# A two-network kernel on one core: the entry's norm ahead of the filter's layers, the latent's tiles ahead of the context's behind the even product, modulation halves ahead of their weight units

## The reference

```python
for layer in range(DEPTH):                 # 0 even, 1 odd
    sh, sc, ga = adaln(c or c_ctx, w_mod[layer], b_mod[layer])   # silu(cond) @ w_mod + b_mod, in three parts
    h = rms_norm(x, g_pre[layer]) * (1 + sc) + sh                # for the latent and for the context
    # even: h @ e_w_in -> Hyena branch (short convolution, long convolution with a filter made by
    #       a small sine network, sin(freq * (z @ w1 + b1)) and so on), and attention with rotary q, k
    # odd:  h @ o_w_in -> q, k, v, o, z of an mLSTM
    y = mixer(h) @ w_out
    x = x + ga * rms_norm(y, g_post[layer])
```

## Time and profile before

| | us |
|---|---|
| median of 3 runs (lowest, highest) | 2029.33 (2027.41, 2030.05) |
| the profiled execution, own time | 2031.51 |
| its span, first to last instruction | 2029.7 |
| PE busy | 1884.0 |
| DVE busy | 1129.2 |
| ACT busy | 857.6 |
| mean granted clock of PE | 0.961 |

### The profile page before, as it was taken

One profiled execution on the slowest core, in us unless ns is written; L12 is line 12 of the kernel. 1 busy time (PEld: TensorE's weight loads), 2 busy tenths in 40 slices (PEclk: granted clock), 3 DMA queues, 4 the chain that ended last, 5 costly groups with the idle time before them and its releaser, 6 DMA issues. The chain is left out here.

```text
span 2029.7 us, 24208 instructions
## 1 busy us (share of the span) xinstructions
PE 1884.0 (93%) x9322; PEld 1512.7 (75%) x9322; DVE 1129.2 (56%) x2019; ACT 857.6 (42%) x1353; POOL 48.9 (2%) x53
## 2 busy tenths in 40 slices
PE   5999999899897889997878999999999999999997
PEld 2666688777685767885557788879987878779986
DVE  3534266566533733346985677566654667466644
ACT  3313345312223533254444465645643555635542
POOL 1000000000000000001000001000000001000000
PEclk8989999999998989998889999999999999999999
DMA  9305511211233422264004434455555444445552
GB/s 333 136 32 193 201 54 51 73 62 42 82 106 115 145 79 83 87 200 149 1 1 166 162 113 152 145 166 166 187 187 187 155 134 135 145 165 168 187 197 83
DMA packets 113786, 265.12 MB, mean 131 GB/s; under 512 B 4695, under 2 KB 8056, under 8 KB 113480
## 3 DMA queue, kind: packets, MB, share of 16 engines
q1 hardware_dynamic: 109408, 248.47, 37.0%
q0 software_dynamic: 3008, 10.85, 1.6%
q10 hardware_dynamic: 1256, 4.25, 0.6%
HBM read 262.51 MB, written 1.05 MB: 130 GB/s over the span
## 5 line engine op out<-in xcount | busy, mean ns | idle before, releaser
L144 DVE TENSOR_TENSOR qw_rest<-weights,qw_lead 128x1024 fp32r<-128x1024 f32 (+2 forms) x428 | 520.5, 1218 | 584.3 <-ACT qw_lead L309 583.5
L309 ACT ACTIVATE qw_lead<-weights 128x1024 fp32r<-128x1024 f32 (+2 forms) x428 | 448.3, 1049 | 706.0 <-PE psum L153 671.9
L153 PE MATMUL psum<-qw_lead,b_h_lead 128*128 128x512 f32 (+1 forms) x480 | 199.5, 416 | 10.1 <-DVE hT L2682 5.4
L153 PE MATMUL psum<-qw_lead,b_h_rest 128*128 128x512 f32 (+1 forms) x480 | 188.8, 393 | 0.0
L153 PE MATMUL psum<-qw_rest,b_h_lead 128*128 128x512 f32 (+1 forms) x480 | 188.3, 392 | 0.0
L153 PE MATMUL psum<-e_h_lead,qw_lead 128*128 128x512 f32 x320 | 144.8, 453 | 6.0 <-PEq L118 5.7
L153 PE MATMUL psum<-b_h_lead,qw_lead 128*128 128x256 f32 x512 | 145.2, 284 | 0.0
L153 PE MATMUL psum<-b_h_rest,qw_lead 128*128 128x256 f32 x512 | 144.9, 283 | 0.0
L153 PE MATMUL psum<-b_h_lead,qw_rest 128*128 128x256 f32 x512 | 144.9, 283 | 0.0
L153 PE MATMUL psum<-e_h_lead,qw_rest 128*128 128x512 f32 x320 | 126.7, 396 | 0.0
L153 PE MATMUL psum<-e_h_rest,qw_lead 128*128 128x512 f32 x320 | 125.9, 393 | 0.0
(11 more groups left out here) (460 smaller groups left out, 3533.2 us busy)
## 6 DMA issues: line engine op xcount, KB each, us to landing
weights<-in_w_in SPq DMA_DIRECT2D x48, 1024.0 KB, 5.0
weights<-in_o_w_in SPq DMA_DIRECT2D x32, 1024.0 KB, 5.3
weights<-in_w_mlp_up SPq DMA_DIRECT2D x32, 1024.0 KB, 5.5
weights<-in_w_mlp_down SPq DMA_DIRECT2D x32, 1024.0 KB, 4.8
weights<-in_e_w_in SPq DMA_DIRECT2D x26, 1024.0 KB, 5.2
weights<-in_w_mod SPq DMA_DIRECT2D x24, 1024.0 KB, 6.6
weights<-in_e_w_out SPq DMA_DIRECT2D x8, 1024.0 KB, 4.8
weights<-in_o_w_out SPq DMA_DIRECT2D x8, 1024.0 KB, 4.9
```

The source lines that it names most:

```text
L144: return eng.tensor_tensor(self.rest[at], src, self.lead[at].bitcast(F32), ALU.subtract)
L153: mm = nc.tensor.matmul(out, l, r, start=start and i == 0, stop=stop and i == 2)
L309: self.core.nc.scalar.activation(self.buf.lead[self.at(u)], self.raw(u), ACT.Copy).then_inc(self.lead_ready, 1)
```

## The change

It does five things, all of them to the order of work.

1. At the entry the first sine, the squares of x, the second sine, the squares of ctx and the root come ahead of the first modulation row's copy on ACT; the second layer's product comes ahead of the second modulation half on PE; the tables' DMAs from POOL wait for the second row and not for the first.
2. In `e_q2` and `e_gatt` each raw half stands ahead of its split unit, not behind it: the places of `mods1` are 15.9 + 2n, `late` is 0.05.
3. In the stream, the first half of `o_q` stands ahead of the four `mod1g` halves; `floor` is now 34.0 from the last unit of `e_out` on.
4. `Residual` and `OddNorm` are cut into pieces with places of their own: the two latent tiles go through square, root, add and norm first; the context's tiles are released from their banks and left until the latent's transposes stand. A Sqrt on a constant comes ahead, at 29.1.
5. The second `Residual`, behind the odd product, uses the same pieces.

```diff
     def cols(name, w, starts, width=BANK, chunks=None):
...
                 for q in range(2):
+                    if chunk:
+                        mod_half(*chunk, q)
                     units.append((at, q * 2 * width, 2, width, True))
-                    if chunk:
-                        l, j = chunk
-                        units.append((len(halves), 0, 4, BANK, False))
...
-    mods("mod1g", 1, (4, 5))
     w = a["o_w_in"][0]
-    cols("o_q", w, (0, 512))
-    cols("o_k", w, (OD_K, OD_K + 512))
+    first["mod1g"] = len(units)
+    first["o_q"], early = len(units) + 4, len(halves)
+    halves.append([(w[0:BANK, 0:BANK].rearrange("(k p) n -> p k n", p=P), 0, 4, BANK)])
+    for j in (4, 5):
+        for r in range(2):
+            mod_half(1, j, r)
+    for h, at in ((early, 0), (early, 1), (len(halves), 0), (len(halves), 1)):
+        units.append((h, at * 2 * BANK, 2, BANK, True))
+    halves.append([(w[BANK:2 * BANK, 0:BANK].rearrange("(k p) n -> p k n", p=P), 0, 4, BANK)])
+    cols("o_q2", w, (512,))
...
@@ Filter.layers, args, sines
-        yield -4.4
+        yield -4.95
...
-            yield (-6.1, -4.3)[i]
+            yield (-6.1, -4.9)[i]
...
-            yield (-4.7, -3.0)[i]
+            yield (-5.5, -4.85)[i]
...
@@ Enter.stats, norms
-            yield (-4.2, -4.1, -2.9, -2.8)[t]
+            yield (-5.2, -5.1, -4.8, -4.75)[t]
...
-        yield -2.6
+        yield -4.65
...
-        yield -2.75
+        yield -4.7
...
-        yield -2.4
+        yield -4.6
...
 class Residual(Stage):
+    def squares(self, act):
+        for t in range(self.tiles):
+            yield self.places[t][0]
+            act.wait_ge(w.chunk, self.dense.product_at(2 * t + 1))
+            if t:
+                act.wait_ge(self.squared, t)
+            nc.scalar.activation(self.junk.rearrange("p (j n) -> p j n", j=2), self.bank(t), ACT.Square, accum_out=self.ssq[:, t:t + 1]).then_inc(self.squared, 1)
+
+    def roots(self, act):
+        yield self.places[0][0] - 1.5
+        self.core.nc.scalar.activation(self.root[:, 0:1], self.core.ident[:, 0:1], ACT.Sqrt)
+        for t in range(self.tiles):
+            yield self.places[t][1]
...
+    def means(self, dve):
+        for t in range(self.tiles):
+            yield self.places[t][1] - 0.05
...
+    def products(self, dve):
+        for t in range(self.tiles):
+            yield self.places[t][2]
...
+    def adds(self, dve):
+        for t in range(self.tiles):
+            yield self.places[t][3]
...
@@ OddNorm.turns
-                pe.wait_ge(self.residual.read, 2 * s + 2)
+                pe.wait_ge(self.residual.read, 2)
...
@@ even_layer, first phase
-    filt.others_first = lambda pool: pool.wait_ge(mods0.rows_out, 1)
+    filt.others_first = lambda pool: pool.wait_ge(mods0.rows_out, 2)
...
-    mods1 = Mods(core, "m1_", r, [(0, 4), (0, 5), (1, 0), (1, 1), (1, 2), (1, 3)], raws, [17.7 + 2 * n for n in range(12)],
+    mods1 = Mods(core, "m1_", r, [(0, 4), (0, 5), (1, 0), (1, 1), (1, 2), (1, 3)], raws, [15.9 + 2 * n for n in range(12)],
...
-    run_stages(core, [... Feed(core, (dense,), (mods0, mods1), prime=(-1.9, -1.2, 3.0), late=(first["e_q2"], 2.1), floor=(first["e_kv"], 3.1)),
+    run_stages(core, [... Feed(core, (dense,), (mods0, mods1), prime=(-1.9, -1.2, 3.0), late=(first["e_q2"], 0.05), floor=(first["e_kv"], 3.1)),
...
@@ even_layer, last phase
+    res = Residual(core, "er_", dense, NT, [0, 0, 1, 1], ...,
+                   [(30.6, 30.7, 30.9, 31.1), (30.8, 31.2, 31.4, 31.6), (31.3, 32.6, 32.7, 34.7), (31.5, 32.9, 33.3, 34.9)], ...)
+    mods2 = Mods(core, "m2_", r, [(1, 4), (1, 5)], ..., [32.1, 32.2, 32.3, 32.4], ..., late=3.0)
+    norm = OddNorm(core, res, odd.h, ...,
+                   st[:, 16:32], [(32.0, 32.2, 32.8), (32.3, 32.5, 33.2), (35.0, 35.2, 35.6), (35.3, 35.5, 35.8)], ((33.5, 0.15), (36.0, 0.3)))
-    run_stages(core, [dense, source, res, norm, mods2, qk, Feed(core, (dense, qk), (mods2,), floor=(where["units"][-3], 33.1)),
+    run_stages(core, [dense, source, res, norm, mods2, qk, Feed(core, (dense, qk), (mods2,), floor=(where["units"][-1], 34.0)),
...
@@ odd_layer, its Residual
+                   [(at, at + 0.6, at + 0.9, at + 0.9), (at + 0.6, at + 1.2, at + 1.5, at + 1.5)])
```

More of the change, by code:

```diff
@@ L1446, in __init__ @@
         self.squared, self.meaned, self.rooted, self.read, self.x_ready = s("squared"), s("meaned"), s("rooted"), s("read"), s("x_ready")
-        self.vector, self.scalar = (self.adds,), (self.squares,)
+        self.vector, self.scalar = (self.means, self.products, self.adds), (self.squares, self.roots)
     def bank(self, t):
@@ new lines, in roots @@
+    def roots(self, act):
[3 more added lines that the diff above has]
+            yield self.places[t][1]
+            act.wait_ge(self.meaned, t + 1)
+            self.core.nc.scalar.activation(self.root[:, t:t + 1], self.mean[:, t:t + 1], ACT.Sqrt).then_inc(self.rooted, 1)
+    def means(self, dve):
+        for t in range(self.tiles):
+            yield self.places[t][1] - 0.05
+            dve.wait_ge(self.squared, t + 1)
+            self.core.nc.vector.tensor_scalar(self.mean[:, t:t + 1], self.ssq[:, t:t + 1], 1.0 / D, EPS, ALU.mult, ALU.add).then_inc(self.meaned, 1)
@@ new lines, in products @@
+    def products(self, dve):
+        core, nc, two = self.core, self.core.nc, lambda z: z.rearrange("p (j n) -> p j n", j=2)
+        for t in range(self.tiles):
+            yield self.places[t][2]
+            dve.wait_ge(self.rooted, t + 1)
+            core.dve_chain(dve, nc.vector.reciprocal(self.rec[:, t:t + 1], self.root[:, t:t + 1]))
+            if t >= 2:
+                dve.wait_ge(self.x_ready, t - 1)
+            nc.vector.scalar_tensor_tensor(out=two(self.tmp[t % 2]), in0=self.bank(t), scalar=self.rec[:, t:t + 1], in1=two(core.ga[:, self.gate_of[t], :]),
+                                           op0=ALU.mult, op1=ALU.mult).then_inc(self.read, 1)
@@ L1601, in even_layer @@
     u = first["e_q2"]
-    items.append(Item(**span(range(u, u + 8, 2), 16.0, 2.0), groups=tokens(BANK), src=r.h, **heads_out(BANK)))
+    items.append(Item(**span(range(u + 1, u + 8, 2), 16.0, 2.0), groups=tokens(BANK), src=r.h, **heads_out(BANK)))
     u = first["e_gatt"]
@@ L1605, in even_layer @@
     for i in range(2):
-        items.append(Item(**span(range(u + 8 * i, u + 8 * i + 8, 2), 24.0 + 8 * i, 2.0), groups=feats, src=r.h,
+        items.append(Item(**span(range(u + 8 * i + 1, u + 8 * i + 8, 2), 24.0 + 8 * i, 2.0), groups=feats, src=r.h,
                           act=lambda g, i=i: silu(4 * i + g)))
@@ L1612, in even_layer @@
     dense = Dense(core, "e_in_", items, (0, 1, 2, 3), outs_ready=x_turned)
-    raws = [first["e_q2"] + 1 + 2 * n for n in range(4)] + [first["e_gatt"] + 1 + 2 * n for n in range(8)]
+    raws = [first["e_q2"] + 2 * n for n in range(4)] + [first["e_gatt"] + 2 * n for n in range(8)]
     def second_free(pe):
@@ L1798, in odd_queries @@
     items = []
-    for name, chan0, dst, width, dt in (("o_q", 0, odd.qT, SEQ, 1.06), ("o_k", 8, odd.kT, 2 * SEQ, 2.0)):
+    for names, chan0, dst, width, dt in (("o_q", "o_q2"), 0, odd.qT, SEQ, 1.06), (("o_k", "o_k2"), 8, odd.kT, 2 * SEQ, 2.0):
         act_out, dve_out = out_of(dst, chan0)
```

87 lines of the change are left out of this document (36 added, 51 removed).

## The result

Median 2052.39 us (2050.97 to 2053.67, four runs) against 2029.03 for the kernel before on the same chip (2027.41 to 2030.05, four runs): ratio 1.0116, 95% interval 1.0098 to 1.0133, or 23.4 us more. The prediction said 2045.5, slower. The direction and the mechanism held, and the size was 7 us short.

The account below looks back on a forecast made before the run. PE was taken as the bound, busy 1884.0 of 2029.7 us. Terms -4.8 + 2.8 + 19.0 + 7.0 - 4.2 - 4.0 + 0.4 = +16.2 us on the median 2029.3 gave 2045.5 us, range 2030 to 2056.

Parts of the forecast that it names:

- The five waits of ACT: First phase: row's copy falls behind a take waiting for a DMA; PE stands 3.9 us in five pairs, 19 us lost.
- Rival A: First phase: the copy is not held, as the half lands within 2.3 us of the sums' start; 2019.5 us, chance 0.15.
- The clock after such stalls: First phase: lower clock behind each 3.9 us stall costs 1.4 us, 7 us lost in all; bounds 0 and 10.
- Rival B: First phase: the stalls come but the clock holds; 2038.5 us, chance 0.2.
- The first raw half waits for the filter: At the filter's end: PE stands 2.8 us at the first raw half, waiting for DVE's last filter step.
- The entry: Kernel start: ACT starts on h at 28.3, 4.8 us earlier; gain no less than 3, no more than 5.5.
- the last turn of the shifts and scales stays at 26.1 to 27.1: Kernel start: first row's copy is delayed, but this later turn on PE keeps its time, 26.1 to 27.1 us.
- The end of that phase: First phase's end: less work behind the last product gains 2.2 us, a PE hardly cooled 2.0 more; together 4.2.
- Behind the even product: After the even product: transposes start 11.6 us earlier, later waits leave some 4 us gain; bounds 1 to 8.
- The second residual: Behind the odd product: root and reciprocal of tile 1 come later, behind DVE's add of tile 0; loss 0.4 us.
- Rival C: Entry and tail give nothing, as late filter tables and waits for the gate eat both; 2054.3 us, chance 0.07.
- rival D: First phase: stalls of half the size, from a DMA alone on the queues, tail at its best; 2028 us, chance 0.1.

Follow-up runs that it names:

- e1: Kernel after with `late` of the first phase 0.3, not 0.05, so the weight half's take stands behind the row's copy: 2030.16 us, ratio 1.0008.
- e7: Kernel after with 22 unused 128x128 products ahead of PE's wait for the row in the first five pairs: 2046.11 us, ratio 1.0082.
- e6: Kernel after with `late` of the first phase 2.1 and DVE's last filter step at 16.35, not 17.0: 2021.24 us, ratio 0.9957.
- e5: Kernel after with `late` of the first phase 2.1, as before, so the take stands behind the row's and heads' copies: 2023.00 us, ratio 0.9969.
- e2: Kernel after with the first phase's part undone (raw halves behind their split units, places 17.7 + 2n, `late` 2.1): 2021.94 us, ratio 0.9958.

## Why the prediction was right in kind and short in size

**The five waits of ACT: right.** 5 x 3.9 - 0.6 = 19.0 us predicted, 19.2 measured (3.6, 3.5, 3.9, 3.7, 4.5). The half's way from the sums to ACT, 6.2 us in the earlier trace rows, took 6.35 in the wait shown (193.19 to 199.54). e1 shows that the order of take and copy makes them: with it turned, none is left. Rival A (the copy isn't held) needed a landing within 2.3 us of the sums' start, and ACT's take never started before 6.15 (6.5, 6.4, 6.35, 6.15, 6.9). From SP's issue to the take it was 5.0 to 5.8 us, 5.2 at the third wait. The Trainium skill (DMA: Bandwidth & Descriptors, Anatomy of one DMA) gives a fit that came to an estimate of 4.4 us and waits of 3.2; the waits measured 3.8 on average, so the row was the better guide, and the fit too low here. The page states that fit for copies issued from GpSimd; these are issued from SP.

**The clock after such stalls: the term that was mis-sized.** Predicted 7 us (1.4 each), bounds 0 and 10; measured 12.4 (1.5 to 3.4 each), beyond the upper bound. The step that failed is "I take 1.4 for each stall of 3.9 us": one stall's price put on all five. The 1.4 came from six products after one wait at 553.96, and for that stall it was right, as the level was back at full directly behind them (two windows of before; the last three numbers are PEclk, DMA share, GB/s):

```profile
553.00:557.00 4.00, 3.04 (x8) 2.42 (x9) 3.69 (x5) 2.89 (x7) 0.00 (x0) 0.57 0.96 370
557.00:560.00 3.00, 3.00 (x15) 2.45 (x14) 0.03 (x1) 0.00 (x0) 0.00 (x0) 1.00 1.03 411
```

The row at 517.91 says 1.6 (5.37 less twice 1.88). But behind the 2.59 us of the earlier trace rows before lost some 2.5, and behind the 10.35 of the earlier trace rows some 2.7. Of the five stalls after, the first two cost what the earlier trace rows shows (1.7 and 1.5), the other three 2.5 to 3.4, since the level stayed low for longer. The third, from 201 us on:

```profile
201.00:208.00 7.00, 6.87 (x20) 5.42 (x20) 4.55 (x7) 0.08 (x1) 0.00 (x0) 0.52 0.07 22
208.00:211.00 3.00, 3.00 (x17) 1.69 (x17) 1.22 (x1) 1.06 (x1) 0.00 (x0) 0.99 0.23 29
```

The length of a wait doesn't tell which price it pays: 3.6 us cost 1.7, and 3.7 cost 2.5. e7 shows the cause. The Trainium skill (TensorE: Matmul & The Clock Gate, Part 1) says that idleness brings the throttled rate back, and the runs agree (that the clock can fall without idle time as well is told below). Rival B (the clock holds) fell.

**The first raw half waits for the filter: right, a little short.** Predicted 2.8 us, measured 3.9. PE came at 135.8 and not at 138.2, since the filter's sums didn't lose the clock this time, and DVE's step ended only 1.6 us earlier than I had it (139.5 against 141.1). e6 shows that DVE's order makes it. What I left out is that the clock was low there before as well (behind L834, 140 to 147 us): by the products' shifts the wait cost 2.5 us net, from -6.1 to -3.6.

**The entry: too much.** Predicted 4.8, measured 3.4 at ACT's first step on h, and 2.8 from 80 us on. In the timeline of PE after:

```profile
20.65 1.87 PE L915 MATMUL psum<-small,e_qT 128*128 128x2 f32 x8 [2.24 <-ACT e_qT L897]
22.45 3.64 PE L887 MATMUL psum<-weights,cond 128*32 128x512 f32 x16
26.80 1.87 PE L915 MATMUL psum<-small,e_qT 128*128 128x2 f32 x8 [0.71 <-ACT e_qT L897]
28.53 1.95 PE L1036 MATMUL psum<-ident,x_res 128*128 128x128 f32 x8
```

Here "the last turn of the shifts and scales stays at 26.1 to 27.1" failed. It starts 0.7 us later, and takes 1.87 us where before, at the full level, it took 1.05. I had named the wait for the first row's copy (behind the root) and not what it does to the second. That copy itself came at 20.0 and not at 19.3: ACT's first square started at 12.0, where I had x land at 11.4. The low level is read from the durations. PEclk is given as 1.00 from 0 to 37 us, yet the matmuls of L153 take 0.63 us each until 36.6, and 0.39 from 37.7 on.

**The end of that phase: nearly.** Predicted 4.2, measured 3.7 (from +29.4 to +25.7). The idle time ahead of the next phase fell from 2.59 to 0.94 us, and the low clock behind it (2.5 us of PE's busy time before, from 241.24 on) is gone. A new wait of 1.1 us at its second step takes a part back. e5 shows that this gain hangs on the early take, as the loss does.

**Behind the even product: right in sum, with another wait than I named.** Predicted 4.0, measured 4.2 (+25.6 to +21.4). In the timeline of PE:

```profile
670.55 3.64 PE L887 MATMUL psum<-weights,cond 128*32 128x512 f32 x32 [2.26 <-issue]
677.50 0.66 PE L1557 MATMUL psum<-ident,hT 128*128 128x128 f32 x4 [3.31 <-DVE hT L1540]
...
691.32 1.13 PE L908 MATMUL psum<-e_qT,small 128*128 128x512 f32 x2 [2.86 <-ACT e_qT L897]
...
695.83 2.08 PE L908 MATMUL psum<-e_qT,small 128*128 128x512 f32 x2 [3.07 <-DVE ga L931]
```

The transposes come 9.2 us behind the last even product (668.3) and not 21.0: 11.8 us earlier, where I had 11.6. Some 7.6 of it is then given back. I had PE wait first for the context's scaling; the row's copy (L897), which stands behind ACT's work for that same norm, came last instead. The wait for the gate's take is 3.1 us; I had 3.4 from the norm to the gate's part (668.0 to 671.4). The four sums took 3.64 us and not 6.3, as the clock was at its full level this time, and nothing came of it: the second norm ended where I had it, and PE waited 3.31 us for it. That the sum came out within 0.2 us is partly luck.

**The second residual: right and small.** DVE's reciprocal of the second tile moved from 1114.50 to 1134.91, 20.4 us, where the products ahead of it were shifted by 20.2: a loss of 0.2, predicted 0.4. Rival C fell with e2, rival D with the five waits at full size.

Together: entry -2.8, the clock at 110 us -3.3, filter +2.5, five waits and the clock +33.0 (19.2, 12.4, and 1.4 of smaller waits and of the start-up of the pipeline), end of the phase -3.7, behind the even product -4.2, and -1.5 in small pieces later (1.2 of it between no. 2000 and no. 3000), which I haven't traced. That is 20.0, the two spans' difference. Without the 3.3 us at 110 us, which is luck of the profiled executions, it comes to 23.3, close to the 23.4 between the medians. Against the 16.2 predicted that is 7.1 more: 5.4 from the clock's price, 2.0 from the entry and 1.4 from smaller waits, less 1.7 in the rest.

## What to carry to other kernels

An instruction that waits for a DMA belongs, in its engine's queue, behind everything that the bounding engine needs before the DMA can have landed; moving it by a quarter of a place gave 22 us here and by two places 29, and the next wait appeared at once at whatever stood behind it in turn. Price a stall of the bounding PE with the clock behind it, and as a range: here 3.8 us of idle time cost 6.3 on average, 5.0 to 7.8. When a reordering has parts, time each alone: one part hid 8 us of gain in the others.

## What the chip did that I had not expected

- The granted clock fell to 0.5 without any idle time of PE. Behind 32 products of one column each (L834) the same stretch lost 0, 1.7 or 3.4 us in the traces of thirteen kernels. So two single traces can differ by 3.4 us there for no reason of an edit.
- A wait of 3.5 us cost 1.5 us of clock, one of 3.7 cost 2.5 and one of 3.9 cost 3.4: nearly equal waits, and prices that differ by a factor of two.
- 22 products of 128x128 on float32 operands showed as 44 records and took 5.1 us, 0.23 us each, where four transposes of the same shape took 0.60 in all. I had sized the filling of e7 by the transposes.
